# Fused two-block transformer kernel: the first modulation units split between VectorE and TensorE, inputs in long runs, and the first expert's gate moved ahead of the slot tables

## The chip, the core and the metric

One NeuronCore of a Trainium2 chip runs the whole program. The metric is the device time of one execution in microseconds. Engines as the profile names them: PE is TensorE (matmuls; PEld its weight loads), DVE is VectorE, ACT is ScalarE, POOL is GpSimd, SP is SyncE, which here only issues DMAs. All data is float32; a float32 matmul stands in the trace as two passes.

## What is computed

512 tokens of width 1024 pass through three residual layers: differential attention, latent attention (MLA), and a block with dilated attention, a convolution and a mixture of 32 experts. Each layer normalizes x and scales and shifts it by a modulation vector, which is a vector-matrix product of silu(c):

```python
mod = jax.nn.silu(c) @ ada_w + ada_b                  # 1024 x 3072
shift, scale, gate = jnp.split(mod[:, None, :], 3, axis=-1)
h = _rmsnorm(x, norm_g) * (1.0 + scale) + shift       # then h @ w_in ...
...
# experts: each token goes to 2 of the 8 experts of one of 4 groups
yb = (silu(xblk @ w_gate[e]) * (xblk @ w_up[e])) @ w_down[e]
```

The change concerns how the first layer's shift and scale (columns 0 to 2047 of mod) are made, how x and these weights come in, and what happens between the routing of the tokens and the first expert.

## The kernel before

**Work and order.** Every engine runs one hand-written list of instructions in order, and semaphores tie the lists together. Weights come in "units" of 512 columns (2 MB), through a ring of three buffers that SP fills (L614); the modulation weights after the first three units come as halves of 1 MB (L621). A unit of modulation weights holds 8 rows of the matrix per partition, so the product is made in two steps: VectorE sums the 8 rows, each weighed by its element of silu(c), into one row per partition (`weigh_unit`, `weigh_half`, L2092 to L2124: 8 operations of 128x512), and TensorE sums over the partitions with four matmuls against a column of ones (`reduce_columns`, L698); VectorE adds the bias (`take_columns`, L2126).

**The start.** SP loads units 0, 1, 2 and the halves of unit 3; ACT's queue loads c, x, the constants, the positions and six small tables. VectorE weighs units 0, 2 and 3. Unit 1 is made on TensorE alone as a row (`row_unit`, L847): 8 matmuls with one column of silu(c) as the weights and 512 columns of the unit moving, then ACT copies the row out and TensorE turns it into columns. ACT squares x (L1487), POOL makes the reciprocal roots (L1747 to L1760), VectorE scales x (`scale_x`, L2071), TensorE transposes it (L878), ACT copies it out (L1495). When shift and scale are there (`affine`, L2154), ACT and VectorE apply them to four of eight blocks each (L1500, L2240), and the first projection begins: L735, called from L889. `stay_warm` (L862) issues matmuls of 128 columns whose result nobody reads. Bias tables come in as rows and are transposed on TensorE: the first before everything else (L873), two more in the first projection (L897 to L901).

**The first expert.** The router's result decides which rows go to which expert. Items (one expert each, 32 in all) are worked through in order; the first three have fixed experts whose weights are loaded ahead. The rows of items 0 and 1 are picked by matmuls with a one-hot matrix (`pick_rows`, L1168, results in two banks of four blocks), flipped and modulated by VectorE (`flip`, L2560), and used by `gate_then_up` (L1231): gate of item 0, then up, then `down` (L1248). In TensorE's list stand, ahead of the gate of item 0: blocks 0 to 3 of the picking, the counts and shared numbers (L1186, L1187), blocks 4 to 7, the table of row ids (L1190 to L1194, waits for parts_ready) and its turned part (L1195 to L1199, waits for ids_found). VectorE's list (`route`, L1994 to L2054) has: the tables' parts, the expert order for SP, the flip of item 0, the row ids, the destinations, the places of the stores; behind it the spreading of the gate vector (L2633 to L2638) and the flip of item 1. SP's loads of items 3 and up wait for the expert order and for item n-3: the gate's load for its gate (gate_read), up's for its up, down's for its down (`load_expert`, L624). POOL gathers the rows of items 2 and up once ids_ready is set (L1797).

Of the kernel before, what the change touches and what calls it, by code (L numbers as in the profile page):

```python
# [14 lines left out]
P = 128  # L15
# [67 lines left out]
K_COLS = K_ORDER + 5  # L83
# [82 lines left out]
def fused_kernel(nc, a, out, xs, ys, table):  # L166

    with ExitStack() as ctx:
# [26 lines left out]
        col1 = sb("col1", [P, R1_ROWS])  # L195
# [6 lines left out]
        silu_c = sb("silu_c", [P, 16])  # L202
# [74 lines left out]
        turn_over = cosT[:, 128:256]  # L277
        slot_hot = mix[:, 1:3, :].rearrange("p a (n s) -> p (a n) s", s=P)
        item_hot = item_cmp[:, 0:2 * TT, :]
        own_id, item_of = cosT[:, 0:2 * TT], cosT[:, 2 * TT:4 * TT]  # L280
# [11 lines left out]
        def summed(n):  # L292

            return n if n > 0 else 1

        def c_loads():
            return [(silu_c[:, 8 * n:8 * n + 8], a[name][0].rearrange("(p k) -> p k", p=P)) for n, name in enumerate(("c", "c_2"))]

        def first_loads():
            return [(k_sb[:, :], a["constants"]), (bufE[:, 0:T].bitcast(I32), a["positions"].to_broadcast([P, T]))]  # L300

        def table_loads():

            loads = []
            rows = lambda name: (a[name][0] if len(a[name].shape) == 2 else a[name]).rearrange("(r c) -> r c", c=P)
            for at_col, table in ((0, R1), (P, R2)):
                for name, r in table.items():
                    src = rows(SOURCES[name])
                    loads.append((bufD[r:r + src.shape[0], at_col:at_col + P], src))
            loads.append((bufD[0:R3_ROWS, 2 * P:3 * P], a["conv_w_2"][0].rearrange("t (c n) -> (t c) n", n=P)))  # L310
# [11 lines left out]
        N_TABLE1 = len(R1)  # L322
        N_REST = len(table_loads()) - N_TABLE1


        s_c = sem("c_loaded")
        s_first = sem("constants_loaded")
        s_table = sem("first_table_loaded")
# [6 lines left out]
        row_copied = sem("second_unit_row_copied")  # L335
# [64 lines left out]
        xg_scaled = sem("rows_scaled")  # L400
# [7 lines left out]
        def source(kind, u):  # L408
            if kind in ("ada0", "ada1"):
                w = a["ada_w0" if kind == "ada0" else "ada_w1"]  # L410
                return w[:, u * W:(u + 1) * W].rearrange("(p k) n -> p k n", p=P)
# [188 lines left out]
        def _(sp):  # L600
            n, halves = 0, 0
# [77 lines left out]
        def _(pe):  # L679
# [18 lines left out]
            def reduce_columns():  # L698

                n = reduced[0]  # L700
                pe.wait_ge(mod_summed, summed(n))
                bank = dve_banks.claim(pe)
                for j in range(4):
                    last = mm(bank[:, j:j + 1], mod_acc(n)[:, j * P:(j + 1) * P], ones[:, 0:1], start=True, stop=True)
                last.then_inc(dve_filled, 1)
                reduced[0] += 1

            def reduce_row():

                n = reduced[0]  # L710
                pe.wait_ge(mod_summed, summed(n))
# [135 lines left out]
            def row_unit():  # L847

                pe.wait_ge(silu_ready, 1)
                pe.wait_ge(w_in[1], unit_arrival(1))  # L850
                bank = tr_banks.claim(pe)
                for k in range(KT):
                    last = mm(bank[0:1, :], silu_c[:, k:k + 1], unit_view(1)[:, k, :], start=(k == 0), stop=(k == KT - 1))
                last.then_inc(tr_filled, 1)
                pe.wait_ge(row_copied, 1)
                bank = dve_banks.claim(pe)
                for j in range(4):
                    last = mm(bank[:, j:j + 1], mod_acc(1)[0:1, j * P:(j + 1) * P], ones[0:1, 0:1], start=True, stop=True)
                last.then_inc(dve_filled, 1)
                reduced[0] += 1  # L860
# [6 lines left out]
            def table_columns(col, n):  # L867
                bank = act_banks.claim(pe)
# [1003 lines left out]
        def _(dve):  # L1872
# [347 lines left out]
            def skip(n):  # L2220

                act_banks.n += n
# [563 lines left out]
```

## Time and profile before

| | us |
|---|---|
| median of 3 runs (1530.29 to 1532.44) | 1530.45 |
| the profiled execution's own time | 1534.45 |
| its span, first to last instruction | 1532.6 |
| TensorE busy in it | 1384.0 (90%) |
| first matmul of the first projection | 45.37 |
| first matmul of the first expert's gate | 1030.90 |

How to read it: times in the rows are us from the span's start. A row of the timeline gives start, duration, engine, source line, operation, output tile and input tile, shapes and count; in brackets how long the engine had been idle and who released it. The chain of waits is the work that ended last, followed back from the end. In the table of stretches PEclk is the granted share of TensorE's 2.4 GHz; its clock is not recorded for the first 28 us of this execution, where the table prints 1.00.

### The profile page before, as it was taken

The page shows a single profiled execution, that of the slowest core. Times are in us where ns is not written, and L with a number is a line of the kernel's source. Part 1 is how long each engine was busy: PE and PEld are TensorE (multiplying, and loading weights), DVE is VectorE, ACT ScalarE, POOL GpSimd, SP SyncE. Part 2 cuts the span into 40 slices and gives each one's busy share as a digit, 9 for nine tenths or more (in the row PEclk, how much of TensorE's full clock was granted, in tenths as well). Part 3 has the DMA queues.
Part 4 walks back from the last instruction along what each step waited for, and adds up shares of the span by engine and source line. Part 5 has one row for each costly group of instructions (what it writes and reads, how often), then busy time and mean ns, then how long its engine had stood idle before and what let it go on. Part 6 is the DMA issues. An engine that isn't in the chain of part 4 may idle for free.

```text
span 1532.6 us, 17693 instructions
## 1 busy us (share of the span) xinstructions
PE 1384.0 (90%) x6714; PEld 700.3 (46%) x6714; DVE 685.9 (45%) x1323; ACT 356.0 (23%) x778; POOL 139.4 (9%) x251
## 2 busy tenths in 40 slices
PE   4999999999999999999999989978996968769795
PEld 2444444555464444664654445455543324233342
DVE  4675524884266723322599945264121112111125
ACT  2433204653220253430500055110000000000001
POOL 3000000010100000000300000013110101011013
PEclk9999999999999999999999989989998989889898
DMA  9773135008276741003334223269999999999995
GB/s 339 268 246 122 55 110 126 5 1 306 68 254 223 245 164 56 0 1 110 137 110 145 75 110 136 85 232 381 413 409 418 419 418 416 416 419 420 423 425 206
DMA packets 86303, 341.53 MB, mean 223 GB/s; under 512 B 10664, under 2 KB 16601, under 8 KB 73545
## 3 DMA queue, kind: packets, MB, share of 16 engines
q1 hardware_dynamic: 73840, 313.54, 52.7%
q0 software_dynamic: 7584, 17.14, 3.8%
q10 hardware_dynamic: 4792, 9.70, 1.8%
q8 instruction: 55, 0.90, 0.2%
q14 instruction: 32, 0.25, 0.0%
HBM read 323.34 MB, written 23.53 MB: 226 GB/s over the span
## 4 chain that ended last, share of the span: by engine, by line
PE 69%; DMA 14%; DVE 10%; issue 3%; ACT 2%; POOL 1%; DVEq 0%; SPq 0%; POOLq 0%; ACTq 0%
PE score_banks L735 14%; PE bank L746 13%; DMA slots<-in_w_exp_up 11%; PE score_banks L1227 9%; PE score_banks L746 5%; PE bank L1254 5%; PE bank L719 3%; PE bank L953 3%; PE bank L908 2%; PE bank L1055 2%; PE score_banks L1241 2%; PE score_banks L1046 2%; DVE bufD L2097 2%; PE score_banks L965 1%; PE bank L969 1%
## 5 line engine op out<-in xcount | busy, mean ns | idle before, releaser
L735 PE MATMUL score_banks<-slots 128*128 128x512 f32 (+1 forms) x584 | 243.3, 574 | 3.0 <-PE score_banks L735 1.5
L1227 PE MATMUL score_banks<-slots,norm_row 128*64 128x512 f32 (+1 forms) x672 | 151.3, 627 | 44.7 <-DMA slots<-in_w_exp_up 44.5
L746 PE MATMUL bank<-slots 128*128 128x512 f32 x416 | 183.2, 594 | 2.2 <-PE bank L746 0.9
L735 PEld LDWEIGHTS score_banks<-slots 128*128 128x128 f32 x584 | 110.4, 191 | 129.6 <-issue 126.8
L2587 DVE TENSOR_TENSOR mix<-probsT,score_banks 128x256 f32<-128x256 f32 (+1 forms) x39 | 14.4, 370 | 280.4 <-ACT probsT L1701 280.4
L1254 PE MATMUL bank<-slots,mix 128*64 128x512 f32 (+1 forms) x864 | 116.9, 481 | 11.5 <-issue 9.5
L746 PEld LDWEIGHTS bank<-slots 128*128 128x128 f32 x416 | 77.5, 190 | 96.6 <-issue 95.0
L1227 PEld LDWEIGHTS score_banks<-slots,norm_row 128*64 128x64 f32 (+1 forms) x672 | 51.0, 147 | 139.2 <-issue 138.2
L1701 ACT ACTIVATE probsT<-score_banks 128x256 f32<-128x256 f32 (+1 forms) x39 | 13.4, 343 | 431.9 <-PE score_banks L1227 371.3
L746 PE MATMUL score_banks<-slots 128*128 128x512 f32 (+1 forms) x256 | 95.2, 527 | 0.3 <-PE score_banks L746 0.3
L2474 DVE SCALAR_TENSOR_TENSOR bufD<-slots,col,bufD 128x512 f32<-128x512 f32 x120 | 80.5, 745 | 0.4
L1254 PEld LDWEIGHTS bank<-slots,mix 128*64 128x64 f32 (+1 forms) x864 | 45.5, 122 | 67.2 <-issue 60.0
L1750 POOL TENSOR_SCALAR pw<-ss 128x1 f32<-128x1 f32 (+3 forms) x25 | 6.6, 263 | 744.8 <-ACT slots L1392 412.8
L2097 DVE SCALAR_TENSOR_TENSOR bufD<-slots,silu_c,bufD 128x512 f32<-128x512 f32 x91 | 68.4, 752 | 4.7 <-DMA slots<-in_w_mod 1.3
L746 PEld LDWEIGHTS score_banks<-slots 128*128 128x128 f32 x256 | 46.4, 190 | 44.1 <-issue 44.1
L2175 DVE TENSOR_TENSOR mix<-bank,gate_row 128x512 f32<-128x512 f32 x24 | 16.6, 692 | 110.6 <-PE bank L746 110.4
L1227 PE MATMUL score_banks<-slots,mix 128*32 128x256 f32 x896 | 54.6, 398 | 11.9 <-DMA slots<-in_w_exp_up 11.9
L953 PE MATMUL bank<-slots 128*128 128x512 f32 x128 | 61.8, 613 | 0.4 <-PE bank L908 0.4
L1804 POOL DMA_INDIRECT bufD<-normed_rows,w_router x30 | 33.9, 1130 | 298.2 <-PE score_banks L1216 280.2
L2097 DVE SCALAR_TENSOR_TENSOR slots<-slots,silu_c 128x512 f32<-128x512 f32 x70 | 52.6, 752 | 8.3 <-DMA slots<-in_w_mod 5.6
L719 PE MATMUL bank<-k_sb,slots 128*128 128x128 f32 x312 | 46.3, 288 | 5.7 <-DVE slots L2545 1.6
L2598 DVE TENSOR_TENSOR bufD<-bank,cosT 128x512 f32<-128x512 f32 x24 | 16.6, 692 | 75.0 <-PE bank L1254 75.0
(383 smaller groups left out, 1809.0 us busy)
## 6 DMA issues: line engine op xcount, KB each, us to landing
slots<-in_w_exp_down SPq DMA_DIRECT2D x32, 2048.0 KB, 33.8
slots<-in_w_exp_gate SPq DMA_DIRECT2D x32, 2048.0 KB, 27.2
slots<-in_w_exp_up SPq DMA_DIRECT2D x32, 2048.0 KB, 32.3
slots<-in_w_in SPq DMA_DIRECT2D x16, 2048.0 KB, 9.0
slots<-in_w_mod SPq DMA_DIRECT2D x24, 1024.0 KB, 5.2
slots<-in_ada_w SPq DMA_DIRECT2D x18, 1024.0 KB, 6.5
slots<-in_w_out SPq DMA_DIRECT2D x6, 2048.0 KB, 8.2
slots<-in_ada_w SPq DMA_DIRECT2D x3, 2048.0 KB, 20.5
```

The source lines that it names most:

```text
L719: last = nc.tensor.transpose(bank[:, i * P:(i + 1) * P], piece, ident)
L735: last = mm(bank[:, cols], w[:, k, lo:lo + P], src[:, k, cols], start=(k == 0), stop=(k == kts - 1))
L746: last = mm(bank[:, 0:cols], features_k[:, t * P:(t + 1) * P], rhs(k), start=(k == 0), stop=(k == kts - 1))
L908: last = mm(psum[banks][r][:, :], rows[:, k, r * P:(r + 1) * P], weights[:, k, :], start=(k == 0), stop=(k == 3))
L953: ins = mm(gate_bank(group)[:, :], hT[:, k, t * P:(t + 1) * P], z_units[u][:, k, :], start=(k == 0), stop=(k == KT - 1))
L1046: mm(bank[:, :], hT[:, 2 * pair + c, t * P:(t + 1) * P], A8[:, 2 * pair + c, :], start=True, stop=False)
L1055: last = mm(bank[:, c * P:(c + 1) * P], pT[:, j * P:(j + 1) * P], C_tok[:, j, h * P:(h + 1) * P], start=(j == 0), stop=(j == TT - 1))
L1227: last = mm(out, rows[:, k, :], e_gu[it.p][:, :, k, c * pc.ff:(c + 1) * pc.ff], start=(k == 0), stop=(k == KT - 1))
L1254: last = mm(psum[6 + pc.bank][c * pc.size:(c + 1) * pc.size, 0:pc.cols], hTe[pc.bank][:, lo:lo + pc.size], e_down[it.p][:, f, c * pc.cols: ...
L1804: gp.indirect_dma_start(xg[it.q][0:it.rows], None, xs[:, :], bass.IndirectOffsetOnAxis(ap=it.row_ids[0:it.rows, 0:1].bitcast(I32), axis=0) ...
L2097: return v.scalar_tensor_tensor(out=acc, in0=w, scalar=c, in1=acc, op0=ALU.mult, op1=ALU.add)
L2474: conv_at[j] = steps(v.scalar_tensor_tensor(out=conv[:, j, :], in0=src, scalar=wcol, in1=conv[:, j, :], op0=ALU.mult, op1=ALU.add))
```

## The change

At the start:

- x and the first modulation weights are given to the kernel in another order, so that each partition's part is one run; c, the first bias table and the other tables are given with feature as the partition, c and the first table inside the constants. The transposes of tables go.
- x is loaded first, on SP's queue. ACT's queue loads the constants and the positions.
- TensorE begins with 30 warm-up matmuls. ACT scales x in VectorE's place.
- Units 1 and 3 are halved: VectorE weighs four of the eight rows, TensorE makes the product of the other four with one column of silu(c) moving (`half_unit`: 16 matmuls). `take_halves` adds both. ACT now applies shift and scale to three blocks, VectorE to five.

At the first expert: the flip is split into halves (`flip_half`), VectorE flips item 0 and spreads the gates ahead of the slot tables; TensorE picks all rows, does the counts and goes on to item 0's gate; the table of row ids and its turned part are made inside item 0's up. The row ids come behind the destinations on VectorE.

```diff
-        def first_loads():
-            return [(k_sb[:, :], a["constants"]), (bufE[:, 0:T].bitcast(I32), a["positions"].to_broadcast([P, T]))]
...
+            sp.dma_start(x[:, :, :], a["x"]).then_inc(s_xin, 16)
             n, halves = 0, 0
...
+            def half_unit(bank, rows, first):
                 for j in range(4):
+                    for k in range(4):
+                        last = mm(bank[:, j:j + 1], rows[:, k, j * P:(j + 1) * P], silu_c[:, first + k:first + k + 1],
+                                  start=(k == 0), stop=(k == 3))
+                return last
...
-            table_columns(0, R1_ROWS)
-            reduce_columns()
-            row_unit()
+            pe.wait_ge(s_first, 16)
+            stay_warm(30)
             pe.wait_ge(xn_ready, TT)
             for k in range(KT):
                 transposes(act_banks, act_filled, [C_tok[:, t, k * P:(k + 1) * P] for t in range(TT)])
-            reduce_columns()
+            bank0, bank1 = dve_banks.claim(pe), dve_banks.claim(pe)
+            reduce_columns(bank0)
+            pe.wait_ge(silu_ready, 1)
+            pe.wait_ge(w_in[1], unit_arrival(1))
+            half_unit(bank1, unit_view(1)[:, 4:8], 4)
+            reduce_columns(bank1, 4)
             stay_warm(6)
-            reduce_columns()
+            bank2, bank3 = dve_banks.claim(pe), dve_banks.claim(pe)
+            pe.wait_ge(mod_in[0], 16)
+            half_unit(bank3, mod_half[0], 0).then_inc(mod_used, 1)
+            stay_warm(4)
+            reduce_columns(bank2)
+            stay_warm(6)
+            reduce_columns(bank3, 4)
             stay_warm(13)
...
+            pick_rows(4, 5, 6, 7).then_inc(rows_picked, 1)
             pe.wait_ge(shared_ready, 1)
...
-            last = pick_rows(4, 5, 6, 7)
...
+            def beside_first_item(m, k):
+                if m == 0 and k == 0:
+                    pe.wait_ge(half_flipped, 1)
+                elif m == 0 and k == BANK_K:
+                    pe.wait_ge(xgT_ready, 1)
+                elif m == 1 and k == 0:
+                    fill_slots()
+                elif m == 1 and k == BANK_K:
+                    turn_slots()
...
+            act.wait_ge(rstd_ready, 1)
+            for t in range(TT):
+                fn(C_tok[:, t, :], x[:, t, :], ACT.Copy, scale=ss[:, t:t + 1]).then_inc(xn_ready, 1)
...
+                flip_half(items[0], 0, half_flipped)
+                spread_gates()
+                flip_half(items[0], 1, xgT_ready)
                 bank = dve_banks.take(dve)
+                chain(v.tensor_copy(order_ids[0:1, :], bank[0:1, SHARED:SHARED + NE]))
+                dve.sem_inc(order_ready, 1)
...
+                dve.wait_ge(slots_made, 1)
+                chain(v.tensor_scalar(raw_ids, psum[4][:, 0:NE], NOBODY, None, ALU.add))
+                dve.sem_inc(ids_found, 1)
+                chain(v.tensor_copy(row_ids.bitcast(I32), raw_ids))
+                flip_half(items[1], 0)
+                flip_half(items[1], 1, xgT_ready)
...
-            weigh_unit(0)
+            weigh_first_unit()
             dve.sem_inc(unit_used, 1)
-            scale_x(0)
-            dve.wait_ge(act_freed, 1)
+            weigh_second_unit()
             take_columns(0, 0, 0, R1["ada_b0"])
...
+            weigh_third_unit(second_unit_done)
+            dve.sem_inc(unit_used, 1)
+            weigh_fourth_unit()
             take_columns(2, 0, 2, R1["ada_b0"])
-            take_columns(3, 0, 3, R1["ada_b0"])
+            take_halves(3, 0, 3, R1["ada_b0"])
```

## Rows read from the trace of the kernel before

**Rows 1.** Busy time by stretch: us, then busy us of each engine, PEclk, DMA share, GB/s.

```profile
core 0: us, PE busy (x) PEld busy (x) DVE busy (x) ACT busy (x) POOL busy (x), PEclk, DMA share, GB/s
45.37:1000.00 954.63, 928.93 (x3274) 479.07 (x3275) 525.37 (x958) 305.61 (x657) 41.24 (x127) 0.99 0.36 124
...
1147.00:1484.00 337.00, 270.65 (x2051) 116.65 (x2053) 57.08 (x127) 18.05 (x53) 39.34 (x36) 0.91 1.01 419
```

**Rows 2.** Chain of waits at the start: start us, us, what.

```profile
22.34 9.74 PE bank L853 x16
...
45.37 27.75 PE score_banks L735 x64
...
73.41 0.21 PE score_banks L899
73.62 0.26 PE score_banks L900
```

**Rows 3.** Timelines of ACT, POOL, VectorE and TensorE in the first 45 us.

```profile
15.03 1.06 ACT L1487 ACTIVATE slots<-x 128x1024 f32<-128x1024 f32 x1 [6.84 <-DMA x<-in_x]
...
19.38 0.25 POOL L1750 TENSOR_SCALAR pw<-ss 128x4 f32<-128x4 f32 x1 [18.08 <-ACT slots L1487]
...
22.16 0.20 POOL L1760 TENSOR_TENSOR ss<-pw 128x4 f32<-128x4 f32 x1
...
14.89 5.47 DVE L2097 SCALAR_TENSOR_TENSOR bufD<-slots,silu_c,bufD 128x512 f32<-128x512 f32 x7
...
42.40 1.91 DVE L2240 TENSOR_SCALAR slots<-slots,aff,mods 128x512 f32<-128x512 f32 x4
...
20.48 1.87 PE L704 MATMUL bank<-k_sb,bufD 128*128 128x1 f32 x8 [0.47 <-DVEq L2106]
...
33.77 3.72 PE L719 MATMUL score_banks<-k_sb,slots 128*128 128x128 f32 x32
...
40.68 1.05 PE L704 MATMUL bank<-k_sb,bufD 128*128 128x1 f32 x8 [0.96 <-DVEq L2119]
```

**Rows 4.** Busy time by stretch, four stretches around changes of the granted clock.

```profile
1018.10:1021.50 3.40, 3.37 (x16) 3.30 (x16) 2.76 (x14) 0.00 (x0) 1.59 (x1) 0.55 0.58 246
...
1028.20:1030.90 2.70, 2.36 (x23) 2.20 (x22) 1.49 (x4) 0.00 (x0) 0.00 (x0) 1.00 0.66 164
...
1031.40:1034.80 3.40, 3.40 (x20) 1.93 (x18) 2.90 (x11) 0.00 (x0) 1.62 (x3) 0.50 0.96 406
...
38.10:41.50 3.40, 2.44 (x22) 2.25 (x21) 2.42 (x5) 0.39 (x1) 0.96 (x1) 1.00 1.05 377
```

**Rows 5.** Busy time by stretch, while the first loads run.

```profile
2.00:4.00 2.00, 0.00 (x0) 0.00 (x0) 0.00 (x0) 0.00 (x0) 0.00 (x0) 1.00 0.73 162
...
10.00:14.00 4.00, 0.00 (x0) 0.00 (x0) 0.00 (x0) 0.00 (x0) 0.00 (x0) 1.00 1.02 402
```

**Rows 6.** Timelines of TensorE, VectorE, SP and POOL from routing to the first expert.

```profile
1024.34 3.84 PE L1173 MATMUL score_banks<-probsT,slots 128*128 128x128 f32 x32
1028.02 1.87 PE L1193 MATMUL bank<-bufD,mix 128*128 128x32 f32 x16
...
1030.90 8.81 PE L1241 MATMUL score_banks<-slots,mix 128*64 128x256 f32 x64
...
1024.11 0.17 DVE L1992 TENSOR_TENSOR sums<-sums,bufD 128x4 f32<-128x4 f32 x1
...
1028.21 0.42 DVE L2575 TENSOR_TENSOR mix<-score_banks,aff 128x256 f32<-128x256 f32 x1 [0.33 <-PE score_banks L1173]
...
1037.51 1.01 DVE L2637 COPY cosT<-norm_row 64x512 f32<-64x512 f32 x2 [0.24 <-DVE inv_sums L2052]
1038.56 1.23 DVE L2637 COPY sinT<-norm_row 32x256 f32<-32x256 f32 x4
...
1041.23 0.41 DVE L2587 TENSOR_TENSOR mix<-probsT,score_banks 128x256 f32<-128x256 f32 x1
...
1036.46 0.36 SPq L632 DMA_DIRECT2D slots<-in_w_exp_gate  x1
...
1032.38 1.11 POOL L1804 DMA_INDIRECT bufD<-normed_rows,w_router  x1 [11.52 <-DVEq L2019]
```

More of the change, by code:

```diff
@@ L1292, in item @@
                     first_sums()
-                pe.wait_ge(xgT_ready, it.n + 1)
-                if unrolled and it.n < GATE_FIRST:
+                if it is not items[0]:
+                    pe.wait_ge(xgT_ready, it.n + 1)
+                if it is items[0]:
+                    gate_then_up(it, beside_first_item)
+                elif unrolled and it.n < GATE_FIRST:
                     gate_then_up(it)
@@ L2557, in _, with spread_gates, flip_half, flip @@
             residual_and_norm(by_expert_block=True)
-            def flip(it, ahead_of=None):
-                if it.n >= PICKED:
-                    dve.wait_ge(xg_read, it.n - PICKED + 1)
-                if ahead_of is not None:
-                    pc = ahead_of.pieces[-1]
-                    dve.wait_ge(gu_done[pc.bank], pc.used + 1)
+            def spread_gates():
+                for size, gate in gates.items():
+                    cols = D * size // P
+                    for c in range(P // size):
+                        rows = slice(c * size, (c + 1) * size)
+                        steps(v.tensor_copy(gate[rows, :], norm_row[rows, c * cols:(c + 1) * cols]))
+                steps.settle()
+            halves_flipped = [0]
+            def flip_half(it, b, done=None):
+                dve.wait_ge(rows_picked, b + 1)
+                ks = slice(b * BANK_K, (b + 1) * BANK_K)
+                rows = xgT(it.q, it.rows)[:, ks, :]
+                raw = psum[b].rearrange("p (k n s) -> p k n s", k=BANK_K, n=PICKED)[:, :, it.n, :]
+                halves_flipped[0] += 1
+                v.tensor_tensor(rows, raw, aff[3][:, ks].unsqueeze(2).to_broadcast([P, BANK_K, it.rows]), ALU.mult).then_inc(xg_scaled, 1)
+                dve.wait_ge(xg_scaled, halves_flipped[0])
+                last = v.tensor_tensor(rows, rows, mods[3][:, ks].unsqueeze(2).to_broadcast([P, BANK_K, it.rows]), ALU.add)
+                if done is None:
+                    chain(last)
+                else:
+                    last.then_inc(done, 1)
+            def flip(it, ahead_of):
+                dve.wait_ge(xg_read, it.n - PICKED + 1)
+                pc = ahead_of.pieces[-1]
+                dve.wait_ge(gu_done[pc.bank], pc.used + 1)
                 rows = xgT(it.q, it.rows)
@@ L2631, in add_last_sums @@
                 dve.sem_inc(x_ready, 1)
-            for size, gate in gates.items():
-                cols = D * size // P
-                for c in range(P // size):
-                    rows = slice(c * size, (c + 1) * size)
-                    steps(v.tensor_copy(gate[rows, :], norm_row[rows, c * cols:(c + 1) * cols]))
-            steps.settle()
-            flip(items[1])
             def prepare_late_items():
```

225 lines of the change are left out of this document (100 added, 125 removed).

## The prediction

> **What bounds the kernel now.** I read four views in this order. First the busy time by stretch [rows 1]: TensorE works 928.9 of the 954.6 us between 45.4 and 1000 us, so whatever moves its first large matmul, L735 at 45.37 us, moves everything up to the router by the same amount. From 1147 to 1484 us the DMA engines are full (1.01, 419 GB/s) and TensorE works 270.7 of 337 us: there the experts' weights set the pace, and the end moves with the moment at which that stream gets going. The change touches the two places ahead of these blocks: the first 45 us, and 1021 to 1043 us.
>
> Second, the chain of waits at the start [rows 2]. It runs through L853, where TensorE makes the whole second modulation unit as a row, 16 passes in 9.74 us, and ends in L735 at 45.37 us. (A float32 matmul stands in the trace as two passes, so 8 products are 16 passes.) Third, the engines' own timelines there [rows 3], for the prices of the pieces. Fourth, the granted clock [rows 4]: two stretches with what TensorE did in them. The profile shows no clock for the first 28 us (it prints 1.00), but one-column passes tell it: 8 of L704 take 1.87 us at 20.48 us and 1.05 us at 40.68 us [rows 3], so the first stood at the lower level, 1.2 GHz, and the second at 2.4 GHz.
>
> **The start, part by part.** *Loads.* x goes out first, on SP's queue, in one run per partition; before, it shared the engines with the first unit and arrived at 15.03 us [rows 3]. x, the larger constants and the positions are 2.10 + 0.39 + 0.26 MB. The engines moved 162 GB/s between 2 and 4 us, then 402 GB/s [rows 5]: 0.32 MB by 4 us and the rest in 6.0 us gives 10.0 us if all three share, and 8.4 us if x goes alone. I take 9.5, nearer to sharing, since both queues are issued at once. Units 0 to 2 (2.10 MB each) follow behind it, at about 15, 20 and 25 us. The long runs themselves I price at no more than the step from 402 to the 419 GB/s of the experts' runs, 4%, and since the units turn out not to be last, at nothing; if they were, 4% of 10 MB would be 1 us.
>
> *Normalizing x.* The squares began at 15.03 us, the reciprocal roots on POOL run from 19.38 to 22.36 us [rows 3]: 4.3 and 3.0 us with the hand-overs, unchanged. The scaling (L2075) goes from VectorE to ScalarE, where a tile of this size took 1.06 us as a square: 4.2 us. It stays behind POOL on ScalarE's queue, and nothing else waits there. The transposes can begin at 9.5 + 4.3 + 3.0 + 4.2 + 0.2 = 21.2 us. That is 12.6 us ahead of the 33.77 us of before, which is the whole point of the new order.
>
> *What TensorE then has to do.* Between the transposes and the first L735 stand, in TensorE's order: 8 one-column passes (unit 0), 32 (its half of unit 1), 8, six warm-up matmuls (12 passes), 32 (its half of unit 3), four warm-ups (8), 8 (unit 2), six (12), 8, thirteen (26). A half unit is 16 products with a 128x128 weight load and one column each. A pass of that kind is paced by the weight load: 0.117 us at the full rate (16 of L1193 in 1.87 us) and 0.216 us at the half rate (8 of L704 in 1.87 us less the tail of the last; 16 of the 128-column L1173 in 3.46 us gives the same) [rows 3, 4, 6]. VectorE's part is 8, 4, 8 and 4 operations of 0.78 us (7 in 5.47 us) [rows 3]; it begins at 15 us and waits for TensorE at each hand-over, so TensorE's chain is the longer one. A wait for silu_ready, for the units or for mod_in is met before TensorE gets there.
>
> *Which rate.* This decides the sign. At 1028.0 us TensorE began 16 passes of 32 columns, went on to 6 of 4 columns (L1197), and was busy 2.36 of 2.7 us; the clock was 1.00 during that, and then 0.50 from 1031.4 to 1034.8 us although dense matmuls had begun [rows 4, 6]. So passes that are nearly all weight load did not keep the clock. Where eight one-column passes stood beside twelve passes of 128 columns, from 38.1 to 41.5 us, it stayed at 1.00 [rows 4]. The change puts 48 one-column passes in a row, 5.6 us of them at the full rate, twice the stretch at 1028 us, with no wide one among them. I take it that the clock falls to 1.2 GHz within that stretch. Behind it six warm-ups (2.6 us at the half rate), then 32 one-column passes, are less wide work than the 3.4 us of L1173, 1018.1 to 1021.5 us, at whose end the clock came back [rows 4]; so I take it to stay down until the thirteen warm-ups at the end.
>
> The Trainium skill ("TensorE: Matmul & The Clock Gate", Terms) says the gate follows how busy TensorE is. By that reading alone the half units would count as work and hold the full rate, the first rival below; the row at 1031.4 us speaks against it.
>
> *The sum.* Transposes: 32 passes, 3.7 us at the full rate [rows 3], 6.9 at the half rate; TensorE has stood idle since the thirty warm-ups that open its program, so 5.3, to 26.5 us. Unit 0: 1.0, to 27.5. Half of unit 1 with its closing passes: 40 passes, 4.7 to 8.6 us, the clock falling on the way, 6.5, to 34.0. Six warm-ups 2.6, to 36.6. Half of unit 3, 32 x 0.216 = 6.9, to 43.5. Four warm-ups 1.7, unit 2 1.7, six warm-ups 2.6, the last reduction 1.7: to 51.2. Then the thirteen warm-ups, 26 passes, 3.2 to 5.6 us, with the clock back before the end: 4.1, to 55.3 us. VectorE's tail (two additions, the affine step, five instead of four blocks) is 3.1 us and ends in that time; four blocks took 1.91 us [rows 3]. So L735 begins at 55.3 in place of 45.37 us: **+9.9 us**. Bounds: 52 with an early x, a late fall of the clock and a short warm-up; 58.5 the other way.
>
> **In the first projection** the turning of two tables goes: L899 and L900, 0.2 and 0.3 us of TensorE [rows 2]: -0.5 us. Their columns now come by DMA over POOL's queue, which is 4 to 5 us earlier with fewer entries; ScalarE needs them hundreds of us later, so that costs nothing.
>
> **The first expert.** Picking rows 4 to 7 (32 passes, 3.84 us) goes ahead of the counts [rows 6]; TensorE is through with both at 1028.2 us, as now. There the gate of item 0 begins at once instead of at 1030.90. Its first four blocks need the flipped first half of the rows: VectorE is done with the row weights at 1024.3, two operations of 0.42 us make it 1025.3; then the spreading of gates moves in (1.01 + 1.23 us), 1027.5; the second half is ready at 1028.5 [rows 6]. No wait. In dense work the clock need not fall as it did at 1031.4. 32 passes of 0.12 us end the gate at 1032.0; now it ends about when SP is let go, 1036.46. Then the moved waits: fill_slots (L1193, 1.9 us) needs parts_ready, which comes behind flips and gates, at 1031.3; half of up follows, to 1035.8; turn_slots needs ids_found, now behind the destination arithmetic, at 1035.8 too, and takes 0.7 us; up ends at 1038.4 instead of 1039.71. Behind these waits only up and what follows it is queued. VectorE has the same operations as now between L1992 at 1024.11 and item 0's product at 1041.23 us, in another order [rows 6]; four waits for TensorE in that stretch go, 1.8 us with the 0.33 ahead of L2575, and splitting the flips costs 0.5: the product starts at 1039.9. So the first down, and items 1 and 2 behind it, come 1.3 us earlier.
>
> SP: the load of item 3's gate goes out at 1032.0 instead of 1036.46 [rows 6], and fills the hole that the DMA engines have then; but up and down of that item wait for up and down of item 0, so the stream as a whole is ahead by those 1.3 us and not by 4.5. **-1.3 us**; bounds 0 (the hole opens again before up) and -3 (the stream keeps more of its lead). POOL: the gather of item 2's rows waits for ids_ready, now 1038.3 against its start at 1032.38 [rows 6]; item 2 is flipped at some 1052 us, so it costs nothing unless the gather lands over 12 us late. The eight scatters behind it end near 1051 instead of 1046 us, 3 us into item 0's store, whose buffer isn't wanted again for tens of us.
>
> Sum: 9.9 - 0.5 - 1.3 = +8.1 us. The profiled execution spans 1532.6 us in a run of 1534.45, 4 us over the median of 1530.45; on the median, **1538.5 us**.
>
> **The rivals.** *Full rate throughout.* If one-column work holds 2.4 GHz: 21.2 + 3.7 + 1.0 + 4.7 + 1.5 + 3.7 + 1.0 + 0.9 + 1.5 + 1.0 = 40.2, VectorE's tail 3.1: 43.3 us, -2.1. With the other terms -3.9: 1526.5, faster. For it: 38.1 to 41.5 us. Against: 1031.4 us. It decides from the point where the second half unit takes under 4 us.
>
> *The clock comes back on the way*, in one of the groups of six warm-ups: then one half unit or the last two reductions run at the full rate, 3 to 5 us less: 1533.5 to 1535.5, and with both groups about 1531. For it: 2.6 us is not far from 3.4.
>
> *The change doesn't bring x forward*, because constants and units share the engines more evenly than I think: x at 12 us, TensorE at the full rate, start 45.8, total within 1.5 us of now: 1529.
>
> **How the numbers follow.** Half rate through 0.54, clock back on the way 0.17, full rate 0.22, late x 0.07. Half rate alone spans 1534.5 to 1542. The measurement tells 0.2%, 3.1 us. The second case is half slower, half within that or nearly so. Faster 0.23, same 0.14, slower 0.63. The range holds all four but the ends: 1525.5 to 1541.5.
>
> **What would show it.** Right: L735 first at 52 to 58 us, the clock's record showing 0.5 from about 30 us, the second half unit over 6 us, item 0's gate read by 1032 us. Wrong: the second half unit in under 4 us at 1.00, and L735 ahead of 45 us; or item 0's up waiting long for VectorE, its product later than 1041.2 us.

## The result and the profile after

| | before | after |
|---|---|---|
| median, us | 1531.45 (1530.29 to 1533.66, 4 runs) | 1543.58 (1543.21 to 1545.36, 4 runs) |
| ratio of the two, 95% interval | | 1.0065 (1.0049 to 1.0081) |
| span of the profiled execution | 1532.6 | 1541.8 |
| first large matmul (L735 before, L720 after) | 45.37 | 54.76 |

By the ratio the change made the kernel slower by 0.65%; the two medians alone give 0.79%, inside the interval. Of all executions in this document one, of a later kernel (the product first, with the start as it was), took 8041 us; it is left out of that kernel's ratio. The chain of waits of the changed kernel at the start, from the chain that ended last (start us, us, what), answers to [rows 2]:

```profile
0.84 9.30 DMA k_sb<-in_constants
...
18.26 4.27 ACT slots L1477 x4
...
22.58 5.38 PE score_banks L704 x32
27.96 0.79 PE bank L689 x8
28.75 3.57 PE bank L837 x32
32.32 0.89 PE bank L689 x8
33.22 2.58 PE bank L844 x12
35.79 6.62 PE bank L837 x32
42.41 1.92 PE bank L844 x8
44.33 1.50 PE bank L689 x8
45.83 2.77 PE bank L844 x12
48.59 1.50 PE bank L689 x8
50.09 4.83 PE bank L844 x26
54.92 5.15 PE score_banks L720 x12
```

L837 is a half unit: 32 passes with a 128x128 weight load and one column moved. The first takes 3.57 us, the second 6.62. L844 is a warm-up matmul of 128 columns and L689 a reduction. From 22.58 us on every step is TensorE's. The same engine by stretch (us, PE busy (x), PEclk, DMA share, GB/s), with the borders at the changes of the granted clock, answers to [rows 4]:

```profile
26.47:33.30 6.83, 6.83 (x64) 1.00 1.01 336
33.30:53.78 20.48, 20.48 (x98) 0.50 1.03 376
```

TensorE is busy for all of 20.48 us and gets 1.2 GHz through all of them. Ahead of the fall at 33.30 us stood 48 one-column passes without a pause, from 27.80 us on. The two long stretches that answer to [rows 1] (us, then busy us of PE, PEld, DVE, ACT, POOL, PEclk, DMA share, GB/s) are what they were, 928.97 us of TensorE in the one and 419 GB/s in the other:

```profile
54.76:1010.05 955.29, 928.97 (x3274) 478.80 (x3273) 525.08 (x957) 304.81 (x655) 41.09 (x127) 0.99 0.35 120
1156.90:1493.90 337.00, 270.96 (x2055) 117.13 (x2056) 57.35 (x127) 18.04 (x53) 39.38 (x36) 0.92 1.01 419
```

I set the matmuls of the two traces side by side, in order, and read by how much the later kernel lags. The lag is 9.4 us at the first large matmul, 9.05 at the end of the first projection (the two tables that are no longer turned), 10.05 at 950 us, 9.86 at item 0's product, 9.2 at the end of the span. The 1.0 us between 800 and 950 us belongs to no edit: the same matmuls met the lower clock at other places (see the last section). So the loss is the start, as a whole.

At the first expert the order of work is the new one. The timelines of TensorE, VectorE and SP there (start us, us, engine, line, tiles, count, idle time before and what ended it) answer to [rows 6]:

```profile
1032.08 6.24 PE L1150 MATMUL score_banks<-probsT,slots 128*128 128x128 f32 x48
...
1038.94 3.67 PE L1234 MATMUL score_banks<-slots,mix 128*64 128x256 f32 x32
...
1034.86 0.42 DVE L2596 TENSOR_TENSOR mix<-score_banks,aff 128x256 f32<-128x256 f32 x1 [0.50 <-PE score_banks L1150]
...
1038.43 0.42 DVE L2596 TENSOR_TENSOR mix<-score_banks,aff 128x256 f32<-128x256 f32 x1 [0.64 <-PE score_banks L1150]
...
1050.17 0.31 DVE L2037 TENSOR_SCALAR inv_sums<-sinT,k_sb 128x24 int32<-128x24 f32 x1
1051.09 0.42 DVE L2626 TENSOR_TENSOR mix<-probsT,score_banks 128x256 f32<-128x256 f32 x1 [0.61 <-DVE inv_sums L2037]
...
1042.81 0.36 SPq L617 DMA_DIRECT2D slots<-in_w_exp_gate  x1
```

Counted from the first pick of rows (1018.13 before, 1028.21 after), item 0's gate is read at 14.40 us where it was read at 18.12, and SP lets the next gate go 3.7 us earlier. But the product (L2626) comes at 22.88 us where it came at 23.09: 0.2 us of the 1.3 that the sum had. VectorE works on the store places (L2037 is their last operation) until 0.61 us ahead of it.

### The profile page after: what moved, and what is told of

Its sections match the earlier page's. It is cut to its first block, busy times and chain, and to the rows that moved or that the text cites. A ratio compares the mean times of both kernels' runs of the same rounds, so it can differ in the third digit from the quotient of the medians.

```text
span 1541.8 us, 17925 instructions
## 1 busy us (share of the span) xinstructions
PE 1402.5 (91%) x6839; PEld 727.6 (47%) x6839; DVE 683.5 (44%) x1324; ACT 358.2 (23%) x777; POOL 136.2 (9%) x245
## 4 chain that ended last, share of the span: by engine, by line
PE 69%; DMA 14%; DVE 9%; issue 3%; ACT 2%; POOL 1%; DVEq 0%; SPq 0%; POOLq 0%; ACTq 0%
PE score_banks L720 14%; PE bank L731 13%; DMA slots<-in_w_exp_up 11%; PE score_banks L1219 9%; PE score_banks L731 5%; PE bank L1247 5%; PE bank L704 3%; PE bank L930 3%; PE bank L885 2%; PE bank L1032 2%; PE score_banks L1234 2%; PE score_banks L1023 2%; PE score_banks L942 1%; PE bank L946 1%; DVE bufD L2492 1%
## 5 line engine op out<-in xcount | busy, mean ns | idle before, releaser
L720 PE MATMUL score_banks<-slots 128*128 128x512 f32 (+1 forms) x584 | 243.3, 574 | 2.7 <-PE score_banks L720 1.9
L720 PEld LDWEIGHTS score_banks<-slots 128*128 128x128 f32 x584 | 110.3, 191 | 129.9 <-issue 127.9
L2626 DVE TENSOR_TENSOR mix<-probsT,score_banks 128x256 f32<-128x256 f32 (+1 forms) x39 | 14.4, 370 | 282.5 <-ACT probsT L1681 281.9
L1219 PE MATMUL score_banks<-slots,mix 128*32 128x256 f32 x896 | 57.9, 416 | 15.7 <-DMA slots<-in_w_exp_up 15.7
L2076 DVE SCALAR_TENSOR_TENSOR bufD<-slots,k_sb,bufD 128x512 f32<-128x512 f32 x90 | 67.7, 752 | 5.4 <-DMA slots<-in_w_mod 2.0
L2076 DVE SCALAR_TENSOR_TENSOR slots<-slots,k_sb 128x512 f32<-128x512 f32 x70 | 52.6, 752 | 8.4 <-DMA slots<-in_w_mod 5.7
L1219 PEld LDWEIGHTS score_banks<-slots,mix 128*32 128x32 f32 x896 | 32.7, 119 | 45.9 <-issue 32.9
```

Of the source, the lines that this page charges most:

```text
L720: last = mm(bank[:, cols], w[:, k, lo:lo + P], src[:, k, cols], start=(k == 0), stop=(k == kts - 1))
L1219: last = mm(out, rows[:, k, :], e_gu[it.p][:, :, k, c * pc.ff:(c + 1) * pc.ff], start=(k == 0), stop=(k == KT - 1))
L2076: return v.scalar_tensor_tensor(out=acc, in0=w, scalar=c, in1=acc, op0=ALU.mult, op1=ALU.add)
```

## The experiments

Theory A is that of the prediction: the one-column products take TensorE's clock down, and TensorE's list at half rate sets the start. Its rivals were that the half units are too much work and too many hand-overs at any clock (B), and that the loads or the new order come too late (C). A second question was where the gain at the first expert went. The median of the kernel before, run beside the experiments on the same chip, was 1534.21 us for the first four kernels, 1533.15 for the next four and 1532.69 for the last.

**The same matmuls with 128 columns moved.** The edit changes nothing but the columns that each product of a half unit moves:

```diff
-    last = mm(bank[:, j:j + 1], rows[:, k, j * P:(j + 1) * P], silu_c[:, first + k:first + k + 1],
+    last = mm(bank[:, j * P:(j + 1) * P], rows[:, k, j * P:(j + 1) * P], k_sb[:, K_C + first + k:K_C + first + k + P],
...
-    chain(v.tensor_tensor(part, bank[:, 0:4], col1[...], ALU.add))
+    chain(v.tensor_tensor(part, bank[:, 0:3 * P + 1:P], col1[...], ALU.add))
```

> The changed kernel with one thing different: each product of the two half units moves 128 columns instead of one. The first of them is the silu column that was moved before, the other 127 are the columns that lie behind it in the constants, and nobody reads their sums; the counts of matmuls, of weight loads, of waits and of warm-ups stay. Theory A (the one-column products take TensorE's clock down to 1.2 GHz, from 33.3 to 53.8 us in the changed kernel, and that is the loss): the granted clock is 1.00 through both half units, the second takes 3.7 to 4.0 us instead of 6.83, the groups of warm-ups and the reductions about half of what they took, and the first L720 comes at 46 to 49 us instead of 54.76; 6 to 9 us off the whole. Theory B (the half units are too many matmuls and hand-overs for TensorE, whatever the clock): the moved columns can only add, first L720 at 54.8 us or later, the whole the same or slower than the changed kernel.

Measured: 1533.96 us, ratio to before 0.9995 (0.9982 to 1.0007). TensorE's timeline and the stretch of both half units (us, PE busy (x), PEclk, DMA share, GB/s):

```profile
28.28 3.82 PE L837 MATMUL bank<-k_sb,slots 128*128 128x128 f32 x32
...
34.17 3.74 PE L837 MATMUL bank<-k_sb,slots 128*128 128x128 f32 x32
...
45.33 16.98 PE L720 MATMUL score_banks<-slots 128*128 128x512 f32 x39 [0.50 <-ACTq L1487]
...
28.28:42.00 13.72, 13.72 (x125) 1.00 1.04 358
```

With 128 times the columns and everything else alike the clock stays at 2.4 GHz, the second half unit takes 3.74 us instead of 6.83 (timeline), and the first large matmul comes at 45.33 instead of 54.76 us: the whole lag of the start is gone, a little more than forecast. This is theory A, and B is out: the number of matmuls, loads of weights and hand-overs is the same.

**Without the warm-ups in the middle.** Three calls of `stay_warm`, of 6, 4 and 6, are taken out.

> The changed kernel without the three groups of warm-ups between its half units and reductions (6, 4 and 6 of them); the 30 at the opening and the 13 at the end stay. Theory A: the clock is down there with them or without, so they only cost what they last, 2.72 + 2.05 + 2.91 us; the second half unit still takes 6.8 us at 0.50, TensorE's list ends 5 to 6 us earlier (VectorE's last weighing ends at 40.2 us and is then nearly last itself), first L720 at 48 to 51 us, whole 4 to 7 us shorter than the changed kernel. The rival (the warm-ups hold the clock up part of the way and earn what they cost): first L720 at 54 us or later.

Measured: 1538.6 us, ratio 1.0019 (1.0005 to 1.0034).

```profile
30.09 5.57 PE L837 MATMUL bank<-k_sb,slots 128*128 128x1 f32 x32
...
37.94 6.96 PE L837 MATMUL bank<-k_sb,slots 128*128 128x1 f32 x32 [0.57 <-DVE mods L2139]
...
53.03 9.18 PE L720 MATMUL score_banks<-slots 128*128 128x512 f32 x21
...
31.60:52.10 20.50, 19.93 (x94) 0.50 1.00 356
```

By the ratios the whole is about 0.5% shorter than the changed kernel, as much as theory A had, but L720 comes only 1.7 us earlier, not 4 to 7. So most of that gain isn't the start's: the two profiled executions lie 5.0 us apart, and the other 3.3 us came behind the start, where nothing was edited. The trace says why the start gained so little. Of the 7.1 us that the warm-ups took from their starts to the next, 1.5 went at the opening, where the first half unit began at 30.09 instead of 28.61 us: POOL and ScalarE handed over 0.8 us later, and the transposes took 6.05 instead of 5.38 us. Another 1.9 went because the clock fell within the first half unit, at 31.6 us, and not behind it (5.57 us instead of 3.71), and 1.5 because its closing ran at the half rate and the second half unit then waited 0.57 us for VectorE to free its bank. So the warm-ups did not bring the clock back, but the list around them is not free to close up either. I had counted only the time of what was removed.

**VectorE weighs all units whole.** The half units go; VectorE has 32 weighings instead of 24, TensorE only reduces, with 6, 6 and 13 warm-ups.

```diff
-            half_unit(bank1, unit_view(1)[:, 4:8], 4)
...
-            half_unit(bank3, mod_half[0], 0).then_inc(mod_used, 1)
...
-                for k in range(4):
+                for k in range(KT):
                     chain(weigh_rows(1, k, unit_view(1)[:, k, :]))
...
-            weigh_fourth_unit()
+            weigh(3)
```

> The changed kernel with the halving undone: VectorE weighs all four units whole, 32 operations, TensorE only reduces them, with groups of 6, 6 and 13 warm-ups between. Long runs, x first, the scaling on ScalarE and the first expert's part stay. Theory A: VectorE sets the start, 16.1 us + 32 x 0.76 + the hand-overs and the tail: first L720 at 46 to 48.5 us, so 6 to 9 us shorter than the changed kernel, and about the 45.37 us of the kernel before. Rival C (what came late is the loads, the constants at 10.1 us and unit 0 at 16.1 against 14.4 us, or the new order, not the half units): first L720 above 52 us here too.

Measured: 1537.11 us, ratio 1.0018 (1.0006 to 1.0031), and L720 at the upper end of the forecast:

```profile
42.42 1.87 PE L689 MATMUL bank<-k_sb,bufD 128*128 128x1 f32 x8 [1.90 <-DVEq L2114]
...
48.48 13.90 PE L720 MATMUL score_banks<-slots 128*128 128x512 f32 x32
...
33.30:47.00 13.70, 9.22 (x41) 0.50 1.05 385
```

VectorE alone, with 8 x 0.76 = 6.1 us more work, has the start 6.3 us earlier than the split at half rate. The loads and the order of this kernel are those of the changed one, as they are in the kernel with 128 columns, which starts at 45.33 us: C is out as the cause of the 9.4 us. The split is ahead of it only with the clock up, 45.33 against 48.48 us. How much of these 3.15 us is the split's isn't shown: in the kernel that weighs whole the clock stood at 0.50 from 33.3 to 47.0 us too, here behind a pause of TensorE, which waited 4.59 us for VectorE until 35.89 us.

**The first expert's part alone.** It is put into the kernel before, whose start stays.

```diff
             pick_rows(2, 3).then_inc(rows_picked, 1)
+            pick_rows(4, 5, 6, 7).then_inc(rows_picked, 1)
...
+                if m == 0 and k == 0:
+                    pe.wait_ge(half_flipped, 1)
...
+                elif m == 1 and k == 0:
+                    fill_slots()
+                elif m == 1 and k == BANK_K:
+                    turn_slots()
```

> The kernel before with the change's part at the first expert alone: picking all rows first, item 0's gate right behind it, counts and slot tables beside it, flips by halves, the new order on VectorE. Its start is that of the kernel before, first L735 at 45.37 us. By the prediction's sum item 0's product comes at 1039.9 instead of 1041.23 us and the whole is 1.3 us shorter. By what the changed kernel's trace shows (product at 1051.09 us, 0.2 us less than the shift it entered this stage with; VectorE's list is busy up to it) the product comes 0.0 to 0.4 us earlier, item 0's gate is read 3 to 4 us earlier all the same, and the whole is shorter by 0 to 0.6 us, the same within what can be told.

Measured: 1532.67 us, ratio 0.9992 (0.9980 to 1.0004): the same. Counted from the first pick the product comes at 22.64 us, 0.45 us earlier than before, a little over the 0.4 that I allowed; 0.18 of it is the picks', which ended earlier. But what follows it gives that back and more, which no theory had:

```profile
1037.14 0.44 PE L1329 MATMUL bank<-k_sb,mix 128*128 128x128 f32 x2 [2.42 <-DVE mix L2632]
1038.14 5.35 PE L1270 MATMUL bank<-slots,mix 128*64 128x512 f32 x16 [0.57 <-ACT mix L1725]
```

The first down takes 5.35 us where the changed kernel's took 3.65: after 2.42 us without work the clock was at 0.50 from 1039.2 us. Item 1's gate begins 1.25 us later than before, counted from the first pick. So moving the gate ahead leaves TensorE a longer pause before the product (2.42 us; 1.98 in the kernel before), and the clock can fall into the next dense work. It need not: the changed kernel had the same pause and kept 3.65 us. The profiled execution of this kernel spans only 1528.4 us, but 4.1 us of that it had gained by the routing, ahead of every edited line.

**The start's order changed on top.** TensorE reduces unit 0 and makes the half of unit 1 ahead of the transposes (38 warm-ups instead of 30, none in the middle), with 128 columns.

```diff
-            stay_warm(30)
-            pe.wait_ge(xn_ready, TT)
-            for k in range(KT):
-                transposes(...)
+            stay_warm(38)
             bank0, bank1 = dve_banks.claim(pe), dve_banks.claim(pe)
             reduce_columns(bank0)
...
             reduce_columns(bank1, 4)
-            stay_warm(6)
+            pe.wait_ge(xn_ready, TT)
+            for k in range(KT):
+                transposes(...)
```

> The kernel with 128 columns in the half units, and TensorE's list at the start in another order: 38 warm-ups instead of 30, then unit 0's reduction and the half of unit 1 with its closing ahead of the transposes instead of behind them, and no warm-ups in the middle. VectorE waited 3.32 us for unit 0's reduction and 1.31 + 1.66 us for later ones. If, as theory A has it, only TensorE's order and rate stood in the way and the loads do not, VectorE goes through its 24 weighings without a wait: 16.0 + 24 x 0.76 + hand-overs, ends at about 35 us, TensorE's list at about 37.5, and the first L720 comes at 40 to 42 us instead of 45.33, whole 3.5 to 5.5 us shorter than with 128 columns alone. The rival (the loads of units 1 to 3 come too late for that order): first L720 at 43.5 us or later, with waits for DMA ahead of a weighing or a half unit.

Measured: 1529.49 us, ratio 0.9973 (0.9962 to 0.9984). The start fell between the two forecasts, because both hold in part: of VectorE's waits for TensorE only the last remains (0.89 us), and waits for loads stand in their place.

```profile
27.01 0.49 DVE L2072 TENSOR_SCALAR bufD<-slots,k_sb 128x512 f32<-128x512 f32 x1 [1.42 <-DMA slots<-in_ada_w]
...
35.00 0.49 DVE L2072 TENSOR_SCALAR bufD<-slots,k_sb 128x512 f32<-128x512 f32 x1 [1.39 <-DMA slots<-in_ada_w]
...
42.52 1.95 PE L720 MATMUL score_banks<-slots 128*128 128x512 f32 x4 [0.50 <-ACTq L1484]
...
29.00:33.00 4.00, 4.00 (x38) 4.00 (x39) 3.54 (x8) 3.15 (x7) 0.00 (x0) 1.00 1.01 292
```

The last line is a stretch (busy us of each engine, PEclk, DMA share, GB/s): 292 GB/s at a full share.

**The product ahead of the store places.** VectorE's operations for the places where results are stored move behind item 0's product. There are nine of them in the code and in the trace; the forecast says ten.

```diff
                 dve.sem_inc(ids_ready, 1)
-                counts_of = table_rows[:, 0:N_WIDE]
...
                 def find_further_items():
+                    counts_of = table_rows[:, 0:N_WIDE]
...
```

> The kernel with the new order of the start, and at the first expert item 0's product put ahead of the places where results are stored (ten operations of VectorE, some 1.9 us with their hand-overs). If VectorE's list is what item 0 waits for, its product comes 1.2 to 1.6 us earlier in the stage, TensorE's idle time before the transposes of the product falls from 2.4 us to about 1, the clock then does not fall ahead of the first down (3.65 us instead of 5.35), and the whole is 1 to 3 us shorter than the one with the new order alone. If the product waits for something else (ScalarE's half of it, up), nothing moves.

> The kernel with 128 columns in the half units and the product first, with the start's order as it was: first L720 at 45.3 us as with 128 columns alone, and the same gain at the first expert as with the new order: product 1.2 to 1.6 us earlier in the stage, first down 3.65 us, whole 1 to 3 us shorter than with 128 columns alone (1533.96 us).

Measured: 1527.47 us, ratio 0.9951 (0.9936 to 0.9966), with the new order; 1533.31 us, ratio 1.0001 (0.9989 to 1.0014), with the start as it was. Rows of the second:

```profile
1042.39 0.42 DVE L2627 TENSOR_TENSOR mix<-probsT,score_banks 128x256 f32<-128x256 f32 x1 [0.83 <-ACT probsT L1681]
...
1042.87 0.44 PE L1306 MATMUL bank<-k_sb,mix 128*128 128x128 f32 x2 [0.94 <-DVE mix L2627]
1043.88 3.65 PE L1247 MATMUL bank<-slots,mix 128*64 128x512 f32 x16 [0.56 <-DVEq L2038]
```

The product now waits for ScalarE's half of it. Counted from the end of the picks it comes 11.3 us behind, instead of 12.8 with 128 columns alone and in the changed kernel. TensorE's pause is 0.94 us, and the first down takes 3.65 us. In the whole the first of the two is 2.0 us shorter than the new order alone, which is at the edge of what can be told, since the two intervals overlap a little (its profiled start came at 43.34 us, with the clock at 0.50 in the last warm-ups). The second misses its forecast: beside the kernel before, its ratio is 1.0001 where 128 columns alone had 0.9995, which can't be told from nothing. Its start came at 47.71 us instead of the 45.3 that I expected of an unchanged start, because the clock was at 0.50 from 22.6 to 29.4 us, through the transposes and the unit 0 reduction. So what it does in the stage is shown, what it is worth in the whole is not.

**The start with 128 columns and the old first expert.**

> The changed kernel's start alone, with 128 columns in the half units, and the first expert's part of the kernel before. First L720 at 45.3 us. Beside the kernel with 128 columns and the whole change, item 0's product comes 0.3 to 0.7 us later in the stage, counted from the routing's first matmul, but the clock has fallen and come back before the first down, which then takes 3.65 us instead of 5.35 us: the whole between 1 us shorter and 0.5 us longer. By the prediction's sum it would be 1.3 us longer.

Measured: 1533.98 us, ratio 1.0003 (0.9992 to 1.0013), against 1533.96 with the whole change (ratio 1.0003 against 0.9995): the first expert's part as it was made is worth nothing that can be told. The product comes 0.9 us later than with it, 0.3 counted from the end of the picks; the first down took 4.84 us here, neither of the two that I gave, since the clock fell a second time, at 1041.3 us. So the order of before isn't free of that fall either. L720 came at 46.30 us.

**The small loads later.** To the new order with the product first, a wait of POOL ahead of its small loads is added.

```diff
             norm_rstd()
+            pool.wait_ge(mod_reduced, 2)
             for dst, src in table_loads():
                 gp.dma_start(dst, src).then_inc(s_in, 16)
```

> The kernel with the new order of the start and the product first, and POOL's fourteen small loads held back until two units are reduced (about 30 us instead of 18 to 26 us). With the new order VectorE waited 1.4 us for unit 2 and 1.4 us for the last half of unit 3, and from 29 to 33 us the DMA engines moved only some 300 GB/s at a full busy share, behind these small loads. If the small loads are what delays the units, the rate stays near 380 GB/s until 34 us, the last half unit is there by 33.7 us, VectorE's second wait falls under 0.5 us, and the first L720 comes at 41 to 42.2 us instead of 42.52 (new order) and 43.34 (new order, product first). If the loads are slow for another reason, VectorE still waits until 34.8 us and the start stays at 42.5 us or later. Either way the whole is 4 to 8 us shorter than the kernel before, since the first expert's part stays.

Measured: 1526.15 us, ratio 0.9955 (0.9939 to 0.9972), profiled span 1524.5 us.

```profile
25.73 0.48 DVE L2074 TENSOR_SCALAR bufD<-slots,k_sb 128x512 f32<-128x512 f32 x1 [0.30 <-DMA slots<-in_ada_w]
...
41.60 3.67 PE L720 MATMUL score_banks<-slots 128*128 128x512 f32 x8 [0.50 <-ACTq L1484]
...
1035.30 3.65 PE L1244 MATMUL bank<-slots,mix 128*64 128x512 f32 x16 [0.57 <-DVEq L2036]
...
29.00:33.00 4.00, 4.00 (x38) 4.00 (x38) 3.21 (x6) 3.18 (x7) 2.86 (x5) 1.00 1.02 392
...
40.00:44.00 4.00, 3.50 (x16) 2.15 (x16) 3.68 (x10) 1.25 (x2) 0.00 (x0) 1.00 1.07 279
```

The rate from 29 to 33 us is 392 instead of 292 GB/s, the second wait for a load is gone and the first is 0.30 us. The low rate has moved with the small loads, which are now issued from 30.13 to 38.6 us: from 40 to 44 us it is 279 GB/s, where the new order alone had 385. The whole is 0.45% under the kernel before and, by the two ratios, about 1.1% under the changed one. The new order alone (0.9973) and the new order with the product first (0.9951) beat both kernels as well. That holding the loads back adds to the latter can be seen in the start, 41.60 us against 42.52 with the new order alone and 43.34 with the product first, and not in the whole.

The first expert's stage in all kernels, in us from the first pick of rows in the same trace. "Half rate until" is the moment at which the granted clock, at 0.50 when the picks began, came back to 1.00:

| kernel | half rate until | picks done | gate begins | gate read | product | first down | item 1's gate begins |
|---|---|---|---|---|---|---|---|
| before | 3.03 | 10.05 | 12.76 | 18.12 | 23.09 | 24.56, takes 3.65 | 28.02 |
| after | 5.19 | 10.11 | 10.73 | 14.40 | 22.88 | 24.36, takes 3.65 | 27.81 |
| 128 columns | 4.12 | 9.60 | 10.22 | 13.89 | 22.37 | 23.85, takes 5.35 | 29.00 |
| no middle warm-ups | 4.17 | 9.62 | 10.24 | 13.92 | 22.39 | 23.87, takes 5.35 | 29.02 |
| VectorE weighs whole | 5.12 | 10.07 | 10.69 | 14.37 | 22.49 | 23.97, takes 3.65 | 27.43 |
| 128 columns, new order | 3.41 | 9.35 | 9.97 | 13.64 | 22.12 | 23.60, takes 5.35 | 28.75 |
| expert's part alone | 4.68 | 9.87 | 10.49 | 14.16 | 22.64 | 24.11, takes 5.35 | 29.27 |
| 128 columns, old expert | 3.45 | 10.25 | 12.97 | 18.33 | 23.30 | 24.91, takes 4.84 | 29.57 |
| product first | 5.04 | 10.04 | 10.65 | 14.33 | 21.32 | 22.80, takes 3.65 | 26.26 |
| new order, product first | 6.03 | 10.51 | 11.13 | 14.80 | 21.80 | 23.28, takes 3.65 | 26.73 |
| and small loads later | 3.29 | 9.29 | 9.91 | 13.58 | 20.58 | 22.06, takes 3.65 | 25.51 |

With the same order, the later the clock comes back in the picks, the later they are done. So kernels are best compared from the end of the picks.

## Why the prediction was right, and where it was off

**The rate.** The deciding step held: the clock fell at the end of the first one-column work, at 33.30 us, and did not come back until 53.78 us, 3.8 us into the thirteen warm-ups. The 128-column kernel, in which only the columns moved differ, shows that they are what took it down. The first rival, full rate throughout, would have needed the second half unit under 4 us; it took 6.83. That rival's own time for the start, 43.3 us, was near enough when the condition was met (45.33 us with 128 columns, of which 1.4 us came with the late opening, next). The rival by which the clock comes back in a group of six warm-ups is out as well: two groups passed within the stretch of 20.48 us.

**The start's sum** came out right, 55.3 us against 54.76, by errors that cancel, which is luck. The transposes began at 22.58, not 21.2 us: the constants, without which ScalarE doesn't start, landed at 10.14 us and not x at 9.5, and POOL's roots took 3.6 + 0.1 us, not 3.0. The first half unit with its closing took 3.57 + 0.89 us, not 6.5: the clock fell only behind it, at 33.30 us. The middle was priced well (half unit 6.62 for 6.9, warm-ups 2.58 and 2.77 for 2.6 each, reductions 1.50 each for 1.7). The last warm-ups took 4.83 for 4.1, since the clock came back only 1 us ahead of their end.

**In the first projection** -0.5 was forecast and the lag fell by 0.3.

**The first expert** is the mis-sized term: -1.3 us forecast, -0.2 measured at the product. The step that failed is that VectorE's list loses four waits and wins no new one. It won 0.50 and 0.64 us ahead of the two flips, which now stand right behind the picks they wait for, and 0.61 us ahead of the product, 1.75 us against the 1.8 that went. Counted from the end of the picks the product came at 13.04 us before and at 12.77 with the change, as in four of the other five kernels with that order (12.42 in the one that weighs whole). It came at 11.28 to 11.29 with the nine operations for the store places moved behind it; the sum hadn't moved them, so this is a further gain and not the forecast one. A smaller miss is the clock in the picks. I had TensorE through picks and counts 10.1 us after the first pick, as before. The clock came back only 5.19 us into the picks, 3.03 before, so the gate began at 10.73 and was read at 14.40, which is 1032.5 in the frame of before and just misses the sign that I gave (1032). Where the clock came back at 3.3 to 3.4 us, the gate began at 9.91 and 9.97. "In dense work the clock need not fall as it did at 1031.4" held for the gate (3.67 us) and failed one step later, in the first down of four of the six kernels that have the change's order on VectorE (5.35 instead of 3.65 us; the changed kernel and the one that weighs whole kept 3.65).

**The loads** of the units I priced as never last. That held in the changed kernel, and failed as soon as TensorE was out of the way: with the new order unit 2 and the last half of unit 3 were 1.4 us late each.

**The whole.** The sum was 8.1 us; the two profiled executions lie 9.2 us apart (1534.45 and 1543.63): 0.5 less at the start, 0.2 more in the first projection, 1.1 more at the first expert, 1.0 more from the clock in the middle, and 0.7 less behind the first expert. The medians lie 12.1 us apart, since the profiled execution of before is 3 us over its median and that of after is on it. The interval of the ratio, 0.49 to 0.81%, is 7.5 to 12.4 us and takes in both. The range of 1525.5 to 1541.5 us around a kernel before of 1530.45 is 0.9968 to 1.0072 as a ratio. The measured ratio, 1.0065, lies in it; the median, 1543.58 us, lies 2.1 us above it, in part since the kernel before took 1531.45 us here.

## What to carry to other kernels

Splitting a vector-matrix product between VectorE and TensorE paid here only where TensorE's part kept its clock; products with one moving column, back to back, lost it here although TensorE was never idle, and moving 128 columns instead of one cost next to no time (3.74 to 3.82 us against 3.71 at the full rate) and kept it. Where work is moved ahead to use an idle engine, look at what the engine then does before its next dense work: behind a pause of 2.42 us the first down took 1.7 us longer in four of five kernels, behind one of 1.98 to 2.06 us it took 1.2 us longer in one of three, and behind one of 0.94 us in none of three. When one limit goes, read the waits of the next engine in the list again before adding up: here they were VectorE's own order, then the loads, then fourteen small loads among the large ones.

## What the runs showed of the chip

- Granted clock with TensorE fully busy: 0.50 for 20.48 us in which 48 of the 98 passes moved one column and the rest were warm-ups of 128, and 1.00 for 13.72 us in which the half units moved 128 columns over the same weights. The Trainium skill ("TensorE: Matmul & The Clock Gate", HAM oscillation — how this bites in real kernels) explains a clock that falls by pauses, in which TensorE waits for loads. The fall at 33.3 us in the kernel that weighs whole agrees, in a pause of 4.59 us (there for VectorE). The changed kernel's trace shows a fall without a pause, TensorE being busy for all of the 6.83 us ahead of it; the measurement decides here.
- The same matmuls far from any edit got different clocks in different kernels. Of the two lines below, the first is the kernel before, the second the one with the expert's part alone, both in the third layer's attention (us, PE busy (x), PEclk, DMA share, GB/s). They hold the same 58 matmuls, 13.7 us of the one and 9.8 us of the other, and the second kernel was 0.6 us ahead in front of them and 4.5 us behind them. One profile of each kernel is therefore no measure of 1 us in the whole; times counted from a point close by in the same stage suffer less.

```profile
905.10:918.80 13.70, 13.57 (x58) 0.50 0.55 232
...
904.48:914.30 9.82, 8.27 (x58) 1.00 0.75 319
```

- DMA engines at a full share moved 292 GB/s from 29 to 33 us while small loads were under way, 392 GB/s there with these loads held back, and 279 GB/s from 40 to 44 us, where they then ran. The Trainium skill ("DMA: Bandwidth & Descriptors", Why small descriptors are slow (HBM only)) gives each packet and descriptor a fixed overhead, whatever its size. In this trace that can't be the whole cause. With the new order, from 29 to 33 us, packets under 2 KB took 6% of the engines' time, while the 8 KB packets of the units took 0.44 us each on average; with the small loads held back they took 0.31 us. Why the large ones took longer isn't shown; no run here varies the size alone.
